# Moving the split of the third weight pair in the up projection of a two-layer trunk, one core

## What is computed

```
h2 = _rmsnorm(x, norm2_g[l]) * (1 + sc2) + sh2
a, b = jnp.split(_dwconv3(h2 @ w_up[l], ffn_conv_w[l]), 2, axis=-1)
x = x + g2 * ((jax.nn.silu(a) * b) @ w_down[l])
```

## Time and profile before

| | before |
|---|---|
| device time, median of 3 runs | 1594.89 us (1594.07 to 1595.28) |
| device time of the profiled execution | 1590.47 us |
| its span, first to last instruction | 1588.7 us |
| TensorE matmuls busy | 1558.7 us, 98% |
| VectorE busy | 1028.6 us, 65% |
| ScalarE busy | 724.5 us, 46% |
| mean granted TensorE clock | 0.994 of full |

### The profile page before, as it was taken

One profiled execution on the slowest core, in us unless ns is written; L12 is line 12 of the kernel. 1 busy time (PEld: TensorE's weight loads), 2 busy tenths in 40 slices (PEclk: granted clock), 3 DMA queues, 4 the chain that ended last, 5 costly groups with the idle time before them and its releaser, 6 DMA issues. The chain is left out here.

```text
span 1588.7 us, 26410 instructions
## 1 busy us (share of the span) xinstructions
PE 1558.7 (98%) x10573; PEld 1454.2 (92%) x10573; DVE 1028.6 (65%) x1659; ACT 724.5 (46%) x1217; POOL 166.9 (11%) x198
## 2 busy tenths in 40 slices
PE   8999999999999999999999999999999999999998
PEld 6678888988999999999987788899899999999998
DVE  6762666737775765757777547676587667476673
ACT  5443454326552543625544344542565355253451
POOL 2000000003211201112000000000221120120210
PEclk9999999999999999999999999999999999999999
DMA  9554010474756957859553521034267585694862
GB/s 360 186 198 159 28 54 27 160 256 110 178 146 157 214 135 169 188 146 206 151 186 108 199 80 54 27 107 133 67 155 184 140 192 147 157 212 137 192 154 84
DMA packets 284511, 236.13 MB, mean 149 GB/s; under 512 B 10698, under 2 KB 254724, under 8 KB 284388
## 3 DMA queue, kind: packets, MB, share of 16 engines
q1 hardware_dynamic: 260064, 189.89, 38.0%
q0 software_dynamic: 24080, 44.45, 16.2%
q10 hardware_dynamic: 244, 0.09, 0.0%
HBM read 188.78 MB, written 3.67 MB: 121 GB/s over the span
## 5 line engine op out<-in xcount | busy, mean ns | idle before, releaser
L1623 ACT ACTIVATE w_hi<-raw_all 128x1024 fp32r<-128x1024 f32 x120 | 126.2, 1056 | 235.1 <-DMA raw_all<-raw_all 105.0
L2210 DVE TENSOR_TENSOR w_lo<-raw_all,w_hi 128x1024 fp32r<-128x1024 f32 x120 | 146.6, 1221 | 117.6 <-ACT w_hi L1623 117.3
L1227 PE MATMUL ps<-gg,w_hi 128*128 128x322 f32 x704 | 218.5, 310 | 0.0
L1229 PE MATMUL ps<-gg,w_lo 128*128 128x322 f32 x704 | 218.2, 310 | 0.0
L1228 PE MATMUL ps<-gg,w_hi 128*128 128x322 f32 x704 | 218.1, 310 | 0.0
L667 POOL DMA_DIRECT2D raw_all<-raw_all x160 | 136.7, 869 | 622.0 <-DMA raw_all<-in_w_up_dram 494.7
L1172 PE MATMUL ps<-hc_lo,w_hi 128*128 128x322 f32 x640 | 199.5, 312 | 0.0
L1170 PE MATMUL ps<-hc_hi,w_hi 128*128 128x322 f32 x640 | 198.9, 311 | 0.0
L1174 PE MATMUL ps<-hc_hi,w_lo 128*128 128x322 f32 x640 | 198.6, 310 | 0.0
L1170 PE MATMUL ps<-ht_hi,w_hi 128*128 128x322 f32 x480 | 150.7, 314 | 5.0 <-ACT s L1641 4.9
L2105 DVE SCALAR_TENSOR_TENSOR x<-ps,modv,x 128x128 f32<-128x128 f32 (+2 forms) x240 | 90.4, 433 | 90.8 <-PE ps L1229 53.2
(11 more groups left out here) (234 smaller groups left out, 3476.7 us busy)
## 6 DMA issues: line engine op xcount, KB each, us to landing
raw_all<-in_w_up_dram SPq DMA_DIRECT2D x280, 256.0 KB, 3.8
raw_all<-raw_all POOLq DMA_DIRECT2D x160, 256.0 KB, 4.1
raw_all<-in_w_in_dram SPq DMA_DIRECT2D x48, 512.0 KB, 5.0
raw_all<-in_w_mod_dram SPq DMA_DIRECT2D x48, 512.0 KB, 4.4
raw_all<-in_w_down_dram SPq DMA_DIRECT2D x16, 768.0 KB, 4.4
raw_all<-in_w_down_dram SPq DMA_DIRECT2D x16, 640.0 KB, 4.2
mod_q<-in_w_mod_dram SPq DMA_DIRECT2D x8, 1024.0 KB, 8.2
raw_all<-in_w_out_dram SPq DMA_DIRECT2D x16, 512.0 KB, 4.3
```

Source lines behind the costliest of these rows:

```text
L1227: mm(out, wh[:, k, :], gh, start=k == 0, stop=False)
L1229: ins = mm(out, wl[:, k, :], gh, start=False, stop=k == kf - 1)
L1623: A(whi_b[:, 2 * i:2 * (i + 1), :], src, ACT.Copy).then_inc(up_hi[i], 1)
L2210: V.tensor_tensor(wlo_b[:, pair, :], raw_b[:, pair, :] if i else first_pair(g), whi_b[:, pair, :].bitcast(F32), ALU.subtract).then_inc(up_ ...
```

## The change

In a unit, hi2 and lo2 (the splits of the third weight pair) of the *next* unit stood at the end of the engines' lists, ahead of that next unit. They are now emitted in the unit that uses the pair: on ACT behind the copy s of that unit, on DVE behind the taps (in the first unit of a chunk, where there are no taps, behind the two last `down_add` as before). In the first unit of a chunk ACT did hi2 ahead of s, and now does it behind it. No instruction is added or taken away, and TensorE's, SP's and POOL's lists are the same; what they wait for is the same too.

```diff
@@ -1654,12 +1654,11 @@  (ACT)
-                        if g == s_gates(c)[0]:
-                            up_split_hi(g, 2)
-                        elif prev is not None:
+                        if g != s_gates(c)[0] and prev is not None:
                             c21(prev)
                             centre(prev, 1)
                         snapshot(g, s1, bx, 1, c11_ready, s1_ready)
+                        up_split_hi(g, 2)
@@ -1676,7 +1675,6 @@
                         if nxt is not None:
                             up_split_hi(nxt, 1)
-                            up_split_hi(nxt, 2)
@@ -2270,10 +2268,10 @@  (DVE)
                                 down_add(c - 1, 7)
-                            up_split_lo(g, 2)
                         elif prev is not None:
                             first_taps(prev)
                             last_taps(prev)
+                        up_split_lo(g, 2)
@@ -2293,7 +2291,6 @@
                             up_split_lo(nxt, 1)
                             c12(g)
-                            up_split_lo(nxt, 2)
```

## The result

The changed kernel takes 1612.9 us, median of four runs (1607.6 to 1617.8), against 1594.5 us (1590.6 to 1595.3) before: ratio 1.0118, with a 95% interval of 1.0100 to 1.0135. It is slower by 18.4 us. The prediction had the side right, but its 1600.5 us asked for a third of the loss, and its range ended at 1608.

What follows compares the result with a forecast made beforehand. TensorE, busy 1558.7 of 1588.7 us, was taken to bound the kernel, waiting 4.9 us for s behind a ring of transfers. Idling of 1.3 us a chunk against 0.6, times eight, gave +5.6: 1594.9 to 1600.5 us, range 1591 to 1608.

Steps and rivals of the forecast that it cites:

- from sum5 to hi1: From sum5 landed to hi1 of the next unit, through the load of block 2 and sum2: taken as 8.5 us.
- s of unit 4: Copy s in a chunk's fourth unit: starts at e + 1.75 after the change, idling TensorE 0.5 us.
- e: Moment in a unit when product 1 would end without idling; moves on 12.44 us a unit, s may start 1.25 us later.
- from hi1 to s: Within a unit, hi1, lo1, c12, c21 and centre up to s: 4.8 us with the hops.
- ring of transfers: Units 14 to 15: sum5, load of block 2, sum2, sum5 in turn take 13.3 us a unit, 0.9 us too slow.
- Unit 1: First unit of a chunk: lo2 ends at s + 2.65 instead of 0.53, sum5 of unit 2 lands at e - 0.8; no idling.
- Units 2 to 5: Rest of a chunk: idling 0.5 and 0.45 us in unit 4, 0.4 in unit 5; 1.3 us against 0.6 now.
- from lo2 of unit 2 to sum5 of unit 3: Load 4, issue of sum4, then sum5 landing: 9.9 us, bounds 8.5 and 11.3.
- The count for the kernel before: Lateness of s in units 2 to 4 before the change: 0.5 us idle in unit 4, 4 us in eight chunks; trace 4.9.
- The new wait for u: Unit 4, product 5: ACT does hi2 ahead of p and u, so u is ready at 5.8, due at 5.33: 0.45 us idle.
- The wash: Chain behind lo2 keeps its 9.0 us, idling moves from unit 4's s to unit 5's: 1593 to 1597 us, chance 0.33.
- the faster case: sum5 to hi1 takes 8.0 us, lo2 to sum5 at most 9.0; all 4.9 us of waits go: 1590 us, chance 0.13.

Runs made afterwards that it cites:

- before_thin: Kernel before, from the third up unit of a layer two of seven loads cut to a quarter, waits unchanged, output not the reference's: 1583.4 us against 1590.4, ratio 0.9946.
- after_first: Changed kernel, but in the first unit of each chunk ACT does hi2 ahead of s as before: 1601.4 us against 1594.3 for the kernel before, ratio 1.0039.
- after_buf: Changed kernel, with spare memory for blocks 4 and 5 of units 2 and 4 in half the chunks, freeing loads of lo2: 1600.8 us, ratio 1.0039 to kernel before.
- first_only: Kernel before, but in the first unit of each chunk ACT does s ahead of hi2: 1606.2 us against 1594.2, ratio 1.0069.

## Why the prediction was wrong in size

**The step that failed: from sum5 to hi1.** The side and the path were right: the loads are held by the later lo2, hi1 becomes the late one, and s stands behind it. The size came from one term. The text put s of unit 4 at e + 1.75 (0.9 + 8.5 + 4.8 - 12.44). The eight chunks have it at e + 2.5 to e + 4.7, on the average e + 3.4. Of the three terms, sum5 of unit 3 was put at e + 0.9 and lands at e + 0.9 on the average (SP issues block 2 of unit 4 at once behind it); from hi1 to s the 4.8 us are 4.7; but from sum5 landed to hi1 of the next unit the text took 8.5 from 8.0 and 9.15, without bounds, and it is 9.7 to 10.8 us, on the average 10.2. That is 1.7 us more in each of eight chunks, 13.6 us, about what the forecast fell short by (18.4 - 5.6 = 12.8). What takes longer is sum2 of unit 4: 5.2 to 6.9 us, where the text had 3.85 from the earlier trace rows. The loads of blocks 4 and 5 and the two behind them come behind the hold all together, at 1322 to 1324 us in the chunk shown, just when sum2 is issued. The text took its price from places in the kernel before, where no loads had been held up to come all at once.

**What bounds the kernel: right in place, cause open.** The only waits in the up units were those for s behind hi2 behind the DMA. But the "ring of transfers" alone was named as the 13.3 us, and taking out its wait for sum5 left them. The DMA share of 0.91 in the earlier trace rows stood there as a side remark; before_thin shows that the traffic matters. And the 4.9 us of the earlier trace rows were called the whole that the change can win. Counted from start to start, as TensorE's time has to be, the same eleven waits cost 6.7 us (and the sixteen of the kernel after 22.4, not 19.8), and before_thin, which has none of them, is 7.0 us faster than before.

**Unit 1: dropped from the sum.** The text had hi2 2.1 us later there and sum5 of unit 2 at e - 0.8 instead of e - 2.9, and then dropped the difference, since from unit 3 on the longer chain behind lo2 of unit 2 decided: of two chains it took the later one. But the two run on the same DMA engines. With unit 1 as before (after_first) lo2 of unit 2 ends in the same place in six of the eight chunks, and the same loads are issued behind it, and yet sum5 of unit 3 lands 0.8 us earlier, at e + 0.2 on the average. The transfer in which the two chains meet is sum2 of unit 3: started late, it runs beside the loads of blocks 4 and 5 and takes 4.8 us instead of 3.5 on the average. At s of unit 4 the difference has become 1.1 us, at s of unit 5 1.4. Busy time by unit in the second chunk of layer 1, before, units 1 and 2 (the last columns are clock, DMA share, GB/s):

```profile
1277.60:1290.05 12.45, 12.45 (x86) 12.45 (x85) 8.07 (x11) 7.43 (x12) 2.58 (x3) 1.00 0.87 199
1290.05:1303.54 13.49, 13.49 (x93) 13.49 (x92) 10.03 (x13) 7.84 (x12) 3.40 (x4) 1.00 0.93 221
```

and after, units 1 to 4:

```profile
1293.35:1305.79 12.44, 12.44 (x86) 12.44 (x85) 7.66 (x10) 7.43 (x11) 2.58 (x3) 1.00 0.67 145
1305.79:1318.41 12.62, 12.62 (x87) 12.62 (x86) 9.84 (x13) 7.85 (x13) 3.23 (x4) 1.00 0.86 211
1318.41:1335.34 16.93, 14.24 (x95) 13.71 (x93) 10.34 (x13) 7.93 (x13) 3.63 (x5) 1.00 0.87 190
1335.34:1348.62 13.28, 12.80 (x76) 12.81 (x77) 10.24 (x13) 7.94 (x13) 2.55 (x3) 0.87 0.70 156
```

In unit 1 the share is 0.67 instead of 0.87, 2.5 us less of the DMA engines' time, and this traffic comes later. It can be made up where the later loads are free: in the four chunks of after_buf with spare memory the share in unit 1 is as low (0.65 to 0.69), and together they take no longer than before. In the kernel after units 2 and 3 are held as well, and it isn't made up. Forecast for unit 1: nothing. Measured by after_first: 11 us, or 1.4 us a chunk.

**Units 2 to 5: near, by luck.** Forecast +5.6 us, and that was all for these units; after_first has +7.1 us for them alone. Two errors meet there: from lo2 of unit 2 to sum5 of unit 3 it has 9.15 us on the average, not 9.9, and from sum5 to hi1 of unit 4 9.9, not 8.5.

**The other terms.** In the kernel after, the way from lo2 of unit 2 to sum5 of unit 3 was put at 9.9 us with bounds of 8.5 and 11.3, and is 9.2 to 10.7, on the average 9.8: right, though with the lateness of unit 1 in it, which the text had left out. The count for the kernel before stopped at unit 4, where the one for the kernel after went on to unit 5; carried on in the same way, the former would have given 1.4 us a chunk, more than the 1.3 after. The trace has little of that: s of unit 5 is later against e than s of unit 4 in two of the eight chunks before. The new wait for u was put at 0.45 x 8 = 3.6 us and is 4.5. The wait for s was to be 0.9 x 8 = 7.2 us and is 15.3.

**What was left out: the clock.** The matmuls' own time was to stay at 1558.7 us and is 1569.3. Two of the longest waits are followed by a stretch at half the clock, see below.

**The rivals.** The wash wanted 9.0 us behind lo2 of unit 2, and all eight chunks took more (9.2 to 10.7); the faster case wanted at most 8.1 us from sum5 to hi1 of unit 4, and it took 9.7 at the least. The price of a DMA that the prediction worked out from the Trainium skill's fit (DMA: Bandwidth & Descriptors, Anatomy of one DMA — SWDGE (gpsimd) path; an estimate of 2.6 us for 256 KB) isn't met here, where other transfers run beside it: sum2 took 6.9 us in the chunk shown.

**Open.** What sets the 13.3 us a unit is argued and not isolated: no run frees all the chains at full traffic. after_buf gained more than its four chunks show: the other four were faster too, and the clock differs from run to run, so its 12 us aren't all of the edit.

## What to carry to other kernels

A split, copy or cast that frees a load buffer belongs to the load, not to the product that uses it: before moving one behind other work "because it isn't due yet", look up which transfers wait for it and how busy the DMA engines are in that stretch. Where their share is about 0.9, two held chains of transfers don't run side by side at their old prices: price each transfer with what the hold will make run beside it, and don't let the later of two delays hide the other. Here the accumulating DMA that met the held loads took 5.2 to 6.9 us instead of about 4. And where an instruction is moved, treat the first and the last turn of the loop as places of their own; here undoing the edit in the first turn alone, eight times in the program, took off 11 of the 18 us.

## What the runs showed of the hardware

**Transfers side by side.** In the kernel before the 160 accumulating DMAs of 256 KB take 3.1 to 6.3 us from issue to landing. In the kernel after, the one that four loads of 256 KB meet within 1.5 us of its issue takes 6.9 us.

**The clock.** In the kernel after, two waits of TensorE in the up units are followed by 3.4 us at half the granted clock. Busy time and clock around s of gate 4 in layer 1 (the share of the DMA engines counts each packet where it starts, so it can pass 1 in a short stretch):

```profile
1222.00:1224.00 2.00, 1.90 (x13) 1.62 (x12) 1.31 (x2) 0.66 (x1) 0.53 (x1) 1.00 0.94 141
1224.00:1226.00 2.00, 0.20 (x1) 0.20 (x2) 1.43 (x2) 1.92 (x5) 0.00 (x0) 1.00 1.12 251
1226.00:1228.00 2.00, 2.00 (x11) 2.00 (x11) 2.00 (x4) 2.00 (x4) 0.04 (x1) 0.70 0.90 263
1228.00:1230.00 2.00, 2.00 (x9) 2.00 (x8) 2.00 (x3) 1.45 (x3) 0.81 (x1) 0.50 0.37 65
```

TensorE stands for 2.1 us, starts at the full 2.4 GHz, and a microsecond later is at 1.2 GHz: matmul follows matmul after 0.27 us instead of 0.15. After the wait of 2.9 us that ends at 1335.8 it is at the low clock within 0.2 us. Each stretch costs about 1.7 us on top of the wait. But the length of the wait doesn't decide it. A wait of 2.4 us, the second longest in the up units, ends at 446.4 us and is followed by the full clock:

```profile
444.00:446.00 2.00, 0.10 (x1) 0.00 (x0) 0.89 (x1) 1.92 (x4) 0.00 (x0) 1.00 0.98 212
446.00:448.00 2.00, 1.63 (x11) 1.63 (x12) 1.97 (x3) 2.00 (x4) 0.00 (x0) 1.00 1.07 268
448.00:450.00 2.00, 2.00 (x15) 1.94 (x14) 2.00 (x3) 2.00 (x4) 0.24 (x1) 1.00 0.24 71
```

So are the waits of 1.9 us (it ends at 1544), 1.5 us (663) and 1.4 us (542). What tells the two kinds apart isn't known.

Mean granted clock over the four runs is 0.985 to 0.992 for the kernel after, against 0.989 to 0.996 in 19 runs of the kernel before beside first_only. A part of the difference lies outside the up units: in the profiled executions the kernel after has a clock of 0.51 from 824 to 831 us, 0.66 from 1079 to 1084 and 0.57 from 1144 to 1152, the kernel before 0.57 from 1131 to 1135 and no other such stretch between 400 us and its last 10. With the two stretches in the up units this is about what TensorE's busy time has grown by (10.6 us). Why the clock falls there isn't known.
